# Moving the matmul operands of a two-block transformer by 32 and 160 bytes in SBUF

## The chip, the cores and the metric

One core of a Trainium2 chip runs the whole program. The metric is the device time of one execution in microseconds (us), first instruction to last with what the runtime puts around them. The kernel before took a median of 1004.35 us in three runs (1004.16 to 1005.6). SBUF is addressed here by the byte inside one partition; an "offset of 32 of 128" between two tiles means that their start addresses differ by 32 after division by 128.

## The reference, cut to what matters

The input is 256 tokens of width 1024 in float32. Block one: a norm, one wide input projection, a sparse attention over the 64 best keys and a latent attention with eight heads each, two gated branch projections, an output projection, then a feed-forward layer of width 4096 (`square(relu(h @ w_ff1)) @ w_ff2`). Block two has two layers: a windowed attention with sinks, and one that mixes compressed, selected and windowed keys; each is followed by a gated feed-forward layer of width 2816. A last norm gives the output. Nearly all arithmetic is in dense products of this form:

```python
z = h @ w_in[l]                                            # 1024 -> 3428
x = x + jnp.square(jax.nn.relu(h2 @ w_ff1[l])) @ w_ff2[l]  # 1024 -> 4096 -> 1024
gate, up = jnp.split(h @ w_gu, 2, axis=-1)                 # 1024 -> 5632, twice
return (jax.nn.silu(gate) * up) @ w_down                   # 2816 -> 1024, twice
```

## The kernel before, in words

Every dense product is done to near float32 accuracy out of three products of the faster type float32r: each operand is split into a high part and a low remainder, and `mm3` (L651 to L655) adds high times low-of-the-other, both ways, and high times high. A weight tile (128 output columns, up to eleven chunks of 128 rows) is loaded by SyncE's queue into one of four `raw` slots. ScalarE copies it rounded into one of four `w_hi` tiles (L1361), VectorE subtracts that from the raw tile into one of four `w_lo` tiles (L1988), and TensorE waits for the count of finished `w_lo` tiles. These three run as rings beside each other, with SyncE loads ahead.

In a product by features (`feature_tile`, L657) the weights are the stationary operand, 128 x 128, and the activations move, 128 x 256, in three matmuls a chunk: `w_hi` against the high activations, `w_hi` against the low ones, `w_lo` against the high ones. Each matmul has a weight load of its own, and the load for the next matmul goes on while the present one streams. The activations are `hh`/`hl` (the normalised rows, for the input, gate, query and up projections), `yh`/`yl` (attention output, for the branch and output-of-attention projections), and `hidh`/`hidl` (the hidden layer, for `w_ff2` and the first down projection; chunks of them also hold the merged branches for `w_out`). In a product by tokens (`token_tile`, L676, and `down_rows` of the last down projection) the roles are exchanged: the activations (`ch`/`cl` or `hidh`/`hidl`) are stationary and the weights move, 384 or 512 columns at a time.

Loops over passes of eight or four tiles cover the long stages (`stage_loop`). Besides, TensorE turns tiles with an identity (`ident`, L918, L940, L1210, L1316), makes attention scores (L902, L903: moving `kh`/`kl`, stationary `qs`) and multiplies probabilities (`PT` inside `big`, stationary) with values inside `work` (L930).

SBUF places follow the order in which `sb(...)` is called in `build_program`, one tensor right behind the other in multiples of 32 bytes. Those that matter, with sizes per partition: four `w_hi` and four `w_lo` of 5632 bytes each; `x` and `big`, 8192 each; `hh` and `hl`, 8192 each; then `ident`, `ones` and some forty small tensors, together 15,712 bytes with the last, `gain2`; then `work`, 91,648 bytes, under which `yh`, `yl`, `hidh`, `hidl`, `qs`, `kh`, `kl`, `xc`, `ch`, `cl` and `steps` lie at places that are multiples of 128 bytes from its start. Several short-lived tensors (`y_rows`, `c_vals`, `c_prob`) share the space of `hh` and `hl` and are declared ahead of them.

Of the kernel before, what the change touches and what calls it, by code (L numbers as in the profile page):

```python
# [24 lines left out]
P = 128  # L25
# [187 lines left out]
def build_program(nc, A, out):  # L213
    ctx = ExitStack()
    with ctx:
        def sb(name, shape, dt=F32, where=ctx):
            return where.enter_context(nc.sbuf_tensor(name, shape, dt))
# [18 lines left out]
        c_max = sb("compressed_max", [P, 2, NT * HU], where=s9)  # L236
        c_sum = sb("compressed_sum", [P, 2, NT * HU], where=s9)
        s9.close()
        hh = sb("hh", [P, KC, T], F32R)
        hl = sb("hl", [P, KC, T], F32R)  # L240
        ident = sb("ident_sb", [P, P])
# [42 lines left out]
        gain2 = sb("mid_and_attention_gain", [P, KC])  # L284


        W = 22912
        s1 = ExitStack()
        work = sb("work", [P, W], where=s1)
        s1.close()  # L290
# [35 lines left out]
        s6.close()  # L326
        ctx.enter_context(nc.sbuf_tensor("_work_place", [P, W], F32))

# [2763 lines left out]
```

## Time and profile before

| | |
|---|---|
| median of the runs | 1004.35 us (1004.16 to 1005.6) |
| the profiled execution | 1004.34 us |
| its span, first to last instruction | 1002.5 us |
| TensorE matmuls busy | 978.8 us, 98% of the span |
| VectorE, ScalarE, GpSimd busy | 691.5, 551.7, 193.9 us |
| TensorE clock granted over the span | 0.997 of full speed |
| DMA | 161.80 MB, 161 GB/s |

How to read it: PE is a matmul, PEld a weight load, which overlaps a matmul. The duration of a matmul is a modelled 280 ns or so from start to drain and matmuls overlap one another, so what a matmul costs is read from the distance between two starts, called the pitch below, and not from its duration.

### The profile page before, as it was taken

To read this page: it belongs to the slowest core of one execution; us is meant where nothing else is said; L and a number is where in the kernel's file an instruction comes from. 1 tells how busy PE (TensorE), PEld (TensorE's weight loads), DVE (VectorE), ACT (ScalarE), POOL (GpSimd) and SP (SyncE) were. 2 spreads that over 40 slices of the span, in tenths; PEclk is the share of its full clock that TensorE was granted. 3 is DMA by queue.
4 is the path that set the end of the run, shared out by engine and by line. 5 is a ranking of instruction groups with operands and counts; after the bars stand their busy time and mean duration, and the time that the engine had idled before them with its cause. 6 is when DMAs were issued, how large, how long until landed. Compare 5 with 4: busy or idle time off the path is not lost.

```text
span 1002.5 us, 21791 instructions
## 1 busy us (share of the span) xinstructions
PE 978.8 (98%) x8096; PEld 953.0 (95%) x8096; DVE 691.5 (69%) x1308; ACT 551.7 (55%) x1044; POOL 193.9 (19%) x227
## 2 busy tenths in 40 slices
PE   6999999999999999999999999999999999999997
PEld 6998999999999999998999999999999999999886
DVE  6689767777775556888666665567787866666543
ACT  6574674556663445776544454447785654454442
POOL 8000000633343433003111111220200211111000
PEclk9999999999999999999999999999999999999999
DMA  9825323545556556525667658774163476663651
GB/s 263 216 96 169 127 84 128 184 154 187 191 169 203 189 180 190 162 59 153 168 177 194 173 149 227 212 160 143 43 195 101 113 196 176 188 188 110 199 175 63
DMA packets 206004, 161.80 MB, mean 161 GB/s; under 512 B 8643, under 2 KB 193320, under 8 KB 205930
## 3 DMA queue, kind: packets, MB, share of 16 engines
q1 hardware_dynamic: 203066, 154.17, 50.9%
q0 software_dynamic: 2720, 6.56, 3.3%
q8 instruction: 49, 0.80, 0.3%
q14 instruction: 25, 0.20, 0.1%
q10 hardware_dynamic: 144, 0.07, 0.0%
HBM read 158.67 MB, written 2.10 MB: 160 GB/s over the span
## 4 chain that ended last, share of the span: by engine, by line
PE 86%; DVE 7%; ACT 3%; issue 1%; DMA 1%; SPq 1%; ACTq 0%; DVEq 0%
PE bank L653 25%; PE bank L654 25%; PE bank L655 25%; PE bank L930 3%; DVE w_lo L1988 3%; PE bank L918 2%; ACT work L1547 1%; ACT w_hi L1361 1%; PE bank L902 1%; PE bank L903 1%; PE bank L905 1%; DVE work L2198 1%; DMA raw<-w_in_in 1%; ACT big L1561 1%; PE bank L831 0%
## 5 line engine op out<-in xcount | busy, mean ns | idle before, releaser
L1988 DVE TENSOR_TENSOR w_lo<-raw,w_hi 128x1024 fp32r<-128x1024 f32 (+2 forms) x302 | 362.8, 1206 | 184.8 <-ACT w_hi L1361 182.3
L653 PE MATMUL bank<-hh,w_hi 128*128 128x256 f32 x1376 | 393.9, 286 | 4.2 <-DVE w_lo L1988 2.4
L655 PE MATMUL bank<-hh,w_lo 128*128 128x256 f32 x1376 | 389.9, 283 | 0.0
L654 PE MATMUL bank<-hl,w_hi 128*128 128x256 f32 x1376 | 389.9, 283 | 0.0
L1361 ACT ACTIVATE w_hi<-raw 128x1024 fp32r<-128x1024 f32 (+2 forms) x302 | 302.3, 1018 | 132.3 <-PE bank L655 129.6
L653 PEld LDWEIGHTS bank<-hh,w_hi 128*128 128x128 f32 x1376 | 264.0, 192 | 6.5 <-DVE w_lo L1988 5.4
L654 PEld LDWEIGHTS bank<-hl,w_hi 128*128 128x128 f32 x1376 | 264.1, 192 | 0.2
L655 PEld LDWEIGHTS bank<-hh,w_lo 128*128 128x128 f32 x1376 | 264.0, 192 | 0.0
L655 PE MATMUL bank<-hidh,w_lo 128*128 128x256 f32 x496 | 140.2, 283 | 0.0
L654 PE MATMUL bank<-hidl,w_hi 128*128 128x256 f32 x496 | 140.0, 282 | 0.0
L653 PE MATMUL bank<-hidh,w_hi 128*128 128x256 f32 x496 | 139.6, 281 | 0.0
L2940 POOL TENSOR_TENSOR hidl<-work,hidh 128x256 f32 (+1 forms) x76 | 82.3, 1083 | 278.6 <-ACT hidh L1659 278.6
L653 PEld LDWEIGHTS bank<-hidh,w_hi 128*128 128x128 f32 x496 | 94.0, 190 | 0.3
L654 PEld LDWEIGHTS bank<-hidl,w_hi 128*128 128x128 f32 x496 | 93.2, 188 | 0.0
L655 PEld LDWEIGHTS bank<-hidh,w_lo 128*128 128x128 f32 x496 | 93.0, 188 | 0.0
L1659 ACT ACTIVATE hidh<-work 128x256 f32 (+1 forms) x76 | 31.8, 419 | 73.7 <-DVE work L2479 68.8
L1547 ACT ACTIVATE work<-work,mn 128x256 f32<-128x256 f32 (+1 forms) x128 | 56.5, 448 | 5.4 <-DVE mn L2312 5.2
L653 PE MATMUL bank<-yh,w_hi 128*128 128x256 f32 x192 | 54.9, 286 | 0.7 <-DVE yl L2357 0.7
L2991 POOL MEMSET big<- 128x256 f32 x4 | 1.2, 312 | 279.8 <-DVE x L2406 206.0
L655 PE MATMUL bank<-yh,w_lo 128*128 128x256 f32 x192 | 54.2, 282 | 0.0
L654 PE MATMUL bank<-yl,w_hi 128*128 128x256 f32 x192 | 54.1, 282 | 0.0
L1653 ACT ACTIVATE work<-work 128x256 f32<-128x256 f32 x44 | 18.4, 418 | 60.6 <-DVE work L2469 60.6
(338 smaller groups left out, 1331.7 us busy)
## 6 DMA issues: line engine op xcount, KB each, us to landing
raw<-ffn_w_gu_in SPq DMA_DIRECT2D x88, 512.0 KB, 5.0
raw<-w_ff_in SPq DMA_DIRECT2D x64, 512.0 KB, 4.3
raw<-w_in_in SPq DMA_DIRECT2D x24, 512.0 KB, 5.0
raw<-ffn_w_down_in SPq DMA_DIRECT2D x44, 256.0 KB, 3.3
raw<-b_w_in_in SPq DMA_DIRECT2D x14, 512.0 KB, 6.3
raw<-ffn_w_down_in SPq DMA_DIRECT2D x16, 384.0 KB, 4.3
raw<-a_w_qkv_in SPq DMA_DIRECT2D x10, 512.0 KB, 4.6
raw<-ffn_w_down_in SPq DMA_DIRECT2D x16, 320.0 KB, 3.5
```

The source lines that it names most:

```text
L653: pe.matmul(o, ah, bh, start=start, stop=False)
L654: pe.matmul(o, ah, bl, start=False, stop=False)
L655: return pe.matmul(o, al, bh, start=False, stop=stop)
L902: pe.matmul(s_out(u, k)[:, j, :], U["q"](h), U["k"](h)[0], start=True, stop=False)
L918: mm = pe.transpose(o[:, j, c, :], s_buf[u % 2][:, h, rows * c:rows * c + rows], ident[:, :])
L930: mm = pe.matmul(psum[V_BANK][:, HD * h:HD * h + HD], PT[0:rows, h, c, :], U["v"](h, c), start=(c == 0), stop=(c == C - 1))
L1361: act.activation(tile_view(w_hi, n), raw_view(n), ACT.Copy).then_inc(hi_done, 1)
L1547: ins = act.activation(s, s, ACT.Exp, scale=-1.0, bias=mn[:, u % 3, h:h + 1], accum_out=ssum[:, u % 3, h:h + 1])
L1653: act.activation(e_buf[:, (j // 2) % 2, :], g_buf[:, (j // 2) % 2, :], ACT.Sigmoid).then_inc(e_done, 1)
L1659: act.activation(hidh[:, bass.ds(local, 1), :], v_buf[:, (j if name == "ff1" else j // 2) % 2, :].unsqueeze(1), ACT.Copy).then_inc(v_hi, 1)
L1988: dve.tensor_tensor(tile_view(w_lo, n), raw_view(n), tile_view(w_hi, n).bitcast(F32), ALU.subtract)\
L2940: pool.tensor_tensor(hidl[:, bass.ds(local, 1), :], v_buf[:, j % 2, :].unsqueeze(1), hidh[:, bass.ds(local, 1), :].bitcast(F32), ALU.subtr ...
```

## The change

Two tensors are declared that nothing reads or writes. The first, 8 floats, lies ahead of `hh` and moves `hh`, `hl` and all small tensors behind them by 32 bytes. The second, 40 floats, lies ahead of `work` and moves `work`, with all that lies in it, by 160 bytes more, 192 in all. `raw`, `w_hi`, `w_lo`, `x`, `big` and the short-lived tensors declared ahead of `hh` stay. No instruction, wait or transfer is added or taken away.

```diff
         s9.close()
+        sb("_apart_from_weight_rows", [P, 8])
         hh = sb("hh", [P, KC, T], F32R)
         hl = sb("hl", [P, KC, T], F32R)
         ident = sb("ident_sb", [P, P])
...
         gain2 = sb("mid_and_attention_gain", [P, KC])
 
 
+        sb("_work_apart_from_weight_rows", [P, 40])
         W = 22912
         s1 = ExitStack()
         work = sb("work", [P, W], where=s1)
```

## Rows read from the trace of the kernel before

**Rows 1.** Page, part 1: busy time of TensorE's two rows.
```profile
PE 978.8 (98%) x8096; PEld 953.0 (95%) x8096; DVE 691.5 (69%) x1308; ACT 551.7 (55%) x1044; POOL 193.9 (19%) x227
```

**Rows 2.** Page, part 4: the chain that ended last, by engine.
```profile
PE 86%; DVE 7%; ACT 3%; issue 1%; DMA 1%; SPq 1%; ACTq 0%; DVEq 0%
```

**Rows 3.** Waits of TensorE: line, who ended it, us in total, times, longest.
```profile
PE bank L653 <- DVE w_lo L1988: 2.4, 4, 1.4
```

**Rows 4.** Stretch: us, then PE, PEld, DVE, ACT, POOL busy (x), clock, DMA share, GB/s.
```profile
240.00:290.00 50.00, 50.00 (x419) 50.00 (x418) 36.17 (x54) 30.77 (x53) 20.43 (x17) 1.00 0.55 177
296.00:326.00 30.00, 30.00 (x251) 29.93 (x250) 16.52 (x16) 13.72 (x15) 10.02 (x11) 1.00 0.60 199
933.00:963.00 30.00, 30.00 (x130) 24.12 (x129) 13.75 (x12) 13.57 (x14) 1.14 (x1) 1.00 0.61 200
```

**Rows 5.** Matmul groups by form: count | busy us, mean ns | idle before, releaser.
```profile
L653 PE MATMUL bank<-hh,w_hi 128*128 128x256 f32 x1368 | 391.7, 286 | 4.2 <-DVE w_lo L1988 2.4 <-DVE hl L2097 1.5 <-DVE work L2534 0.2
L653 PE MATMUL bank<-hidh,w_hi 128*128 128x256 f32 x496 | 139.6, 281 | 0.0
L653 PE MATMUL bank<-yh,w_hi 128*128 128x256 f32 x192 | 54.9, 286 | 0.7 <-DVE yl L2357 0.7
L653 PE MATMUL bank<-w_hi,hidh 128*128 128x512 f32 x88 | 35.0, 398 | 0.0
```

**Rows 6.** Timeline, moving hh, 24 matmuls apart: start us, modelled duration.
```profile
250.05 0.28 PE L654 MATMUL bank<-hl,w_hi 128*128 128x256 f32 x1
...
252.93 0.28 PE L654 MATMUL bank<-hl,w_hi 128*128 128x256 f32 x1
```

**Rows 7.** Timeline, moving hidh: the 1st, 4th to 7th and 25th start.
```profile
340.53 0.28 PE L653 MATMUL bank<-hidh,w_hi 128*128 128x256 f32 x1
...
340.88 0.29 PE L653 MATMUL bank<-hidh,w_hi 128*128 128x256 f32 x1
341.01 0.28 PE L654 MATMUL bank<-hidl,w_hi 128*128 128x256 f32 x1
341.12 0.28 PE L655 MATMUL bank<-hidh,w_lo 128*128 128x256 f32 x1
341.25 0.28 PE L653 MATMUL bank<-hidh,w_hi 128*128 128x256 f32 x1
...
343.41 0.28 PE L653 MATMUL bank<-hidh,w_hi 128*128 128x256 f32 x1
```

**Rows 8.** Timeline, weights moving 384 wide against ch, 12 matmuls apart.
```profile
85.05 0.34 PE L653 MATMUL bank<-w_hi,ch 128*128 128x384 f32 x1
...
87.13 0.34 PE L653 MATMUL bank<-w_hi,ch 128*128 128x384 f32 x1
```

**Rows 9.** Timeline, scores (kh, kl against qs) behind a pause: 2nd, 10th, 16th.
```profile
704.87 0.28 PE L903 MATMUL bank<-kl,qs 128*128 128x256 f32 x1
...
705.82 0.28 PE L903 MATMUL bank<-kl,qs 128*128 128x256 f32 x1
...
706.54 0.28 PE L903 MATMUL bank<-kl,qs 128*128 128x256 f32 x1
```

**Rows 10.** Timeline, compressor, 60-column weight loads, ten matmuls apart.
```profile
732.31 0.28 PE L1177 MATMUL bank<-w_hi,xc 128*60 128x256 f32 x1
...
733.48 0.28 PE L1177 MATMUL bank<-w_hi,xc 128*60 128x256 f32 x1
```

**Rows 11.** The chain in order of time: start us, us, group; short matmuls.
```profile
700.28 0.88 PE bank L918 x8
...
706.82 3.52 PE bank L930 x32
...
931.22 1.79 PE bank L1316 x16
```

**Rows 12.** ScalarE and VectorE groups that write hh/hl and qs/kl.
```profile
L1630 ACT ACTIVATE hh<-x,cols 128x256 fp32r<-128x256 f32 x24 | 12.1, 504 | 10.3 <-DVE x L2406 5.9 <-DVE x L2408 4.3
L1726 ACT ACTIVATE qs<-work,cols 64x256 fp32r<-64x256 f32 x16 | 8.0, 503 | 4.9 <-DVE work L2534 4.7
```

## Prediction, made before the result was known

> **What bounds the kernel now.** I read the page's busy shares first: matmuls cover 98% of the span and weight loads 95% [rows 1]. The chain that ended last agrees: 86% of it is TensorE, 7% VectorE [rows 2]. Of TensorE's waits, those for a `w_lo` tile, the wait one would fear in a kernel that splits its weights on two other engines, sum to 2.4 us in four cases [rows 3]. The stretches say the same stage by stage: in 50 us of the first feed-forward product VectorE works for 36 and ScalarE for 31, while TensorE has no gap [rows 4]. So the time is set by how many matmuls there are and how far apart their starts are. The reader is not to take "98% busy" for TensorE at its best: a 256-column matmul at 2.4 GHz (the granted clock is 1.00 in these stretches) needs 256 / 2.4 = 106.7 ns of streaming. The starts of 24 matmuls on `hh` lie 252.93 - 250.05 = 2.88 us apart, which is 120.0 ns each [rows 6]. 13.3 ns a matmul, 11%, go somewhere, and only an effect on them can make this change worth anything.
>
> **How often the pitch counts.** Each of the three matmul lines has 1368 records of 128 columns on `hh`, 496 on `hidh` and 192 on `yh` [rows 5]; 2056 x 3 = 6168. With the 24 that load only 48 columns left out, that is 6168 x 0.120 = 740 us of the 1002.5 us span. One ns of pitch is 6.2 us. 0.2% of the kernel, 2 us, about what a measurement can tell from no change, is 0.32 ns of pitch. The last down projection has three lines of 88 matmuls of 512 columns [rows 5], 264 in all; one ns there is 0.26 us.
>
> **Which distances change.** Worked out from the declared sizes, modulo 128, moving address minus stationary address:
> - `hh`/`hl` against weights: the way from `w_hi` to `hh` is 8 x 5632 + 2 x 8192 = 61,440 bytes, a multiple of 128. It is 0 before and 32 after. 1368 x 3 = 4104 matmuls.
> - `hidh` and `yh` against weights: `work` starts 16,384 + 15,712 = 32,096 bytes behind `hh`, 96 beyond a multiple of 128. It is 96 before; 192 bytes more make 288, so 32 after. 688 x 3 = 2064 matmuls.
> - Weights moving against `hidh` or `ch`: 32 before, 96 after. Here the change takes away the very distance that it gives to the others.
> - Scores, `kh` against `qs`: both lie in `work`, 0 before and after.
> - Values against `PT` in `big`: 96 to 32. Identity against tiles in `work`: 32 to 0, against `x` or `y_rows`: 0 to 32.
>
> **What the distance is worth, by the trace of before.** It holds the distances 0 and 96 with activations moving, and 32 only where weights move.
> First, 0 against 96. On `hh` the pitch is 120.0 ns. On `hidh` the starts are uneven: 340.88, 341.01, 341.12, 341.25, so 0.13, 0.11, 0.13 us. But the fourth start behind 340.53 is 0.35 later and the seventh 0.72, and 24 matmuls take 343.41 - 340.53 = 2.88 us [rows 7]: again 120.0 ns. The distance moves single starts by up to 10 ns or so and the mean not at all. Counting by stretch gives the same: 419 matmuls in 50 us on `hh` and 251 in 30 us on `hidh`, where about two of each count reach in from outside [rows 4]: 50 / 417 = 119.9 ns, 30 / 249 = 120.5 ns with a short pause among them. If moving `hh` off distance 0 helped by itself, `hidh` would already show it.
> Second, distance 32. Twelve matmuls of 384 columns take 87.13 - 85.05 = 2.08 us, 173.3 ns each [rows 8]; the streaming is 384 / 2.4 = 160.0, so 13.3 ns are over. That is the same surplus as at 0 and 96 with 256 columns. The streams differ (more columns for one load), so this is a near row and no proof.
> Third, a warning that faster starts exist. Scores at distance 0 behind a pause run eight matmuls in 705.82 - 704.87 = 0.95 us, 118.8 ns, and the next six in 0.72 us, 120.0 ns [rows 9]. Products whose weight loads have 60 columns run at 1.17 / 10 = 117.0 ns with distance 32 [rows 10]. I read this as two limits: the moving stream could go on at 117 to 119 ns, and a stream of full weight loads, slowed by the moving reads beside it, settles at 120.0. A weight load without a full stream beside it needs 3.52 / 32 = 110.0 ns with values moving at distance 96, 0.88 / 8 = 110 ns for turns at distance 32 and 1.79 / 16 = 112 ns at distance 0 [rows 11]. So the load alone hardly cares for the distance, and beside a full stream it costs some 9 ns more.
>
> I take 0 ns for the 6168 matmuls, by the nearest rows: two distances with 256 columns and one with 384 all leave 13.3 ns. The bounds: below, the load's own pitch of 111 ns, 9 ns less, -56 us; above, a pitch of 125, 5 ns more and one rounding of the timeline below the widest single step in rows 7, +31 us. Neither end has a steady stretch behind it.
>
> The Trainium skill bears on this at one place, "SBUF - State Buffer", section "SBUF: two separate sides": only the port pair that VectorE and GpSimd share causes contention, and TensorE never waits on anyone; "TensorE: Matmul & The Clock Gate" adds, in its part on what happens when a matmul is issued, two independent read ports, one for the moving operand and one for weight loads. By these pages the distance could not matter, and the sum would be 0. The first half of it the trace doesn't support so plainly, since 9 ns go between the load's pitch alone and beside a full stream; that a distance changes it is shown by no row here.
>
> **The last down projection.** Its distance goes from 32 to 96. The stretch of 30 us holds 130 records [rows 4], less one or two that reach in: 30 / 128.5 = 233 ns, 20 ns over 512 / 2.4 = 213.3. The 384-column surplus of 13.3 ns is the nearest row for another value, so between -7 and +7 ns x 264: -1.8 to +1.8 us. I take 0.
>
> **Small matmuls.** Some 384 on values and 300 turns by identity run at 110 to 112 ns at all of 0, 32 and 96 [rows 11]; up to 2 ns x 700 is 1.4 us either way. I take 0.
>
> **Other engines.** ScalarE and VectorE read and write the shifted tiles too. The copy with a gain into `hh`, which starts at 0 of 128 counted from the weights, takes 504 ns, the one into `qs`, which starts at 96, 503 ns [rows 12]. So 1 ns at most, and 24 copies into `hh` make nothing of it. Every start stays a multiple of 32 bytes, so no transfer changes its packets. `raw`, `w_hi` and `w_lo` don't move, and these carry the work that follows TensorE most closely: 36 of 50 us for VectorE [rows 4]. If the pitch fell to 118, eight-chunk tiles would come every 24 x 118 = 2.83 instead of 2.88 us, still far above what VectorE needs, so a gain would not be caught there.
>
> **Sum.** 0 + 0 + 0 on the profiled execution: span 1002.5 us, 1004.3 with the 1.8 us around it. It equals the median of 1004.35.
>
> **The rivals.**
> - *Distance 32 lets the weight load past the moving stream (faster).* Then the load stops setting the pace and the moving stream does, at 117.0 [rows 10] to 118.8 ns [rows 9], say 117.9: 2.1 x 6168 = -13 us, 991 us. For it: such a pace exists, and the 60-column row that shows it is at distance 32. Against it: that row has half the load, and the 384-column row at 32 keeps its 13.3 ns. A gain on `hh` alone would be -9 us. 0.38 for this family.
> - *Distance 32 makes the starts uneven without paying back (slower).* At 96 every wide step is paid back by a narrow one, and six take 0.72 us [rows 7]. If one 10 ns step of six is not paid back, the pitch is 121.7: 1.7 x 6168 = +10 us, 1014 us. It decides from 0.32 ns of pitch. Place: every tile of every dense stage. For it: single steps do depend on the distance. Against it: no steady stretch in the trace is above 120.0. 0.17.
> - *The change does less than it says.* Scores stay at 0, the 512-column products go from 32 to 96. This ends inside no change, at -1.8 to +1.8 us, and is in its chance.
>
> **How the numbers follow.** No change 0.45, faster 0.38, slower 0.17. The time is that of no change, 1004.3 us; its own range is 1002.3 to 1006.3. Down, the range takes in the faster rival with its larger variants, to a pitch of 117.0: 3.0 x 6168 = 18.5 us, 986 us. Up it reaches to 1010 us, a pitch of 120.9, which takes in the milder part of the slower rival and not its priced middle. About 0.05 is left below and 0.1 above.
>
> **What would show it right or wrong.** Right: 24 matmuls on `hh`, and 24 on `hidh`, still take 2.88 us; the groups of rows 5 keep their counts, and stretches as long as those of rows 4 hold 417 and 249 starts. Faster: 24 take 2.83 us or less in both stages, and the chain keeps its TensorE share of 86%. A change of `hh` alone would mean that 0 is the bad distance. Slower: 24 take over 2.89 us with steps of 125 ns. Wrong in its whole argument: the pitch keeps to 120.0 and the time moves by more than 2 us, for then the difference lies in waits at stage changes, and [rows 3] would show other lines.

## The result, and the profile after

The changed kernel takes a median of 987.01 us (986.34 to 988.08, four runs) beside 1004.3 us before (1004.16 to 1005.6, four runs): 17.3 us less, a ratio of 0.983 with a 95% interval of 0.981 to 0.984. The span of its profiled execution is 986.3 us, 16.2 us less than before. The forecast was no change, 1004.3 us; the faster rival, given 0.38, was the one that came. The time lies inside the stated range of 986 to 1010 us, one us from its lower end, which was there for that rival's largest variant.

The page of the changed kernel: the busy shares, then the chain that ended last by engine. They answer to [rows 1] and [rows 2]; every line number behind the two strips is higher by 1 or 2.

```profile
PE 961.3 (97%) x8096; PEld 935.3 (95%) x8096; DVE 690.9 (70%) x1308; ACT 551.7 (56%) x1044; POOL 195.3 (20%) x227
PE 86%; DVE 7%; ACT 3%; issue 1%; DMA 1%; SPq 1%; ACTq 0%; DVEq 0%
```

The counts are the same, 8096 matmuls and as many weight loads, and the engines beside TensorE are each as busy as they were to 1.4 us. Only TensorE's two rows fell, the matmuls by 17.5 us and the weight loads by 17.7. So the same instructions stand closer together.

The stretches of the changed kernel (us, then PE, PEld, DVE, ACT, POOL busy with counts, clock, DMA share, GB/s), against [rows 4]:

```profile
235.00:285.00 50.00, 50.00 (x431) 50.00 (x431) 37.30 (x54) 31.20 (x54) 21.29 (x19) 1.00 0.58 189
296.00:326.00 30.00, 30.00 (x256) 29.85 (x256) 16.31 (x17) 12.57 (x13) 11.63 (x12) 1.00 0.66 211
917.00:947.00 30.00, 30.00 (x131) 24.14 (x130) 13.94 (x12) 13.80 (x15) 1.15 (x1) 1.00 0.63 203
```

In 50 us on `hh` there are 431 records where there were 419, in 30 us on `hidh` 256 where there were 251, and in the last down projection 131 where there were 130. The granted clock is 1.00 in all, as before.

The timeline shows the pitch itself. First two starts on `hh` that are 24 matmuls apart, then two on `hidh` 24 apart, then two with weights moving 384 wide, 12 apart; they answer to [rows 6], [rows 7] and [rows 8]:

```profile
245.31 0.28 PE L655 MATMUL bank<-hh,w_hi 128*128 128x256 f32 x1
...
248.11 0.28 PE L655 MATMUL bank<-hh,w_hi 128*128 128x256 f32 x1
...
599.93 0.28 PE L655 MATMUL bank<-hidh,w_hi 128*128 128x256 f32 x1
...
602.73 0.28 PE L655 MATMUL bank<-hidh,w_hi 128*128 128x256 f32 x1
...
84.66 0.34 PE L655 MATMUL bank<-w_hi,ch 128*128 128x384 f32 x1
...
86.74 0.34 PE L655 MATMUL bank<-w_hi,ch 128*128 128x384 f32 x1
```

24 matmuls take 2.80 us instead of 2.88 in both: 116.7 ns each instead of 120.0. The 384-column products keep their 2.08 us, although their distance went from 32 to 96 of 128. The scores stay at 120 ns, eight starts in 693.79 - 692.83 = 0.96 us, and the 60-column loads at 117 ns, 1.17 us for ten; rows that answer to [rows 9] and [rows 10]:

```profile
692.83 0.28 PE L905 MATMUL bank<-kl,qs 128*128 128x256 f32 x1
...
693.79 0.28 PE L905 MATMUL bank<-kl,qs 128*128 128x256 f32 x1
...
719.60 0.28 PE L1179 MATMUL bank<-w_hi,xc 128*60 128x256 f32 x1
...
720.77 0.28 PE L1179 MATMUL bank<-w_hi,xc 128*60 128x256 f32 x1
```

Averaged over all steady stretches (starts with no pause in between) the pitch is 116.7 ns on `hh`, 117.0 on `hidh` and 117.1 on `yh`, where all three had 120.0; the 512-column products went from 234.2 to 233.3.

**The ledger.** 4104 x 3.3 + 1488 x 3.0 + 576 x 2.9 + 264 x 1.0 ns = 13.5 + 4.5 + 1.7 + 0.3 = 20.0 us. The span fell by 16.2. The two traces have the same matmuls in the same order, so the distances between starts can be compared one by one: the steady stretches gained 17.2 us and the short runs of matmuls 1.8, while 1.0 was lost near the start to the clock and 1.9 to longer waits and pauses. First the clock. Stretches of before, then of after:

```profile
30.00:36.00 6.00, 6.00 (x111) 5.78 (x111) 5.69 (x13) 2.93 (x8) 1.17 (x2) 0.81 0.91 218
31.00:32.00 1.00, 1.00 (x46) 1.00 (x43) 1.00 (x2) 0.98 (x3) 0.00 (x0) 1.00 0.80 217
37.00:38.00 1.00, 1.00 (x10) 1.00 (x10) 0.00 (x0) 0.83 (x2) 0.00 (x0) 0.93 0.93 96
```
```profile
30.00:36.00 6.00, 6.00 (x107) 5.90 (x107) 5.69 (x13) 2.82 (x7) 1.17 (x2) 0.60 0.92 221
31.00:32.00 1.00, 1.00 (x43) 1.00 (x40) 1.00 (x2) 0.98 (x2) 0.00 (x0) 0.57 0.81 205
37.00:38.00 1.00, 1.00 (x6) 1.00 (x6) 0.00 (x0) 0.00 (x0) 0.00 (x0) 0.52 0.98 94
```

From 30.1 to 32.4 us TensorE runs 90 very short matmuls for the bias table, with 33 of 128 rows in use, and in both executions its clock drops from 2.4 to 1.2 GHz for a while. In the changed kernel the low level lasts from 31.1 us, in the middle of these matmuls, to 38.0; before it lasted from 33.7, behind them, to 37.1. The mean granted clock of the 6 us is 0.60 instead of 0.81. The 250th matmul starts at 35.3 us instead of 34.4. It need not be owed to the change: the four executions of the changed kernel have a mean granted clock of 0.995, 0.995, 0.997 and 0.997, for the kernel before it ranges from 0.994 to 1.000, one execution at 0.989 apart, and the kernel with both at 64, below, has no drop there in its profile. About 1.1 us more goes into waits for weights:

```profile
PE bank L655 <- DVE w_lo L1990: 3.5, 6, 1.4
```

It was 2.4 us in four waits [rows 3]; the other 0.8 us is in many smaller ones. The last 1 us of the difference to the ledger is a price set too high: the ledger gives every matmul the gain of a steady stretch, and the short runs of matmuls, many of them between attention steps, gained less.

### The profile page after: what moved, and what is told of

It is laid out like the page before. It is cut to its first block, busy times and chain, and to the rows that moved or that the text cites. A ratio compares the mean times of both kernels' runs of the same rounds, so it can differ in the third digit from the quotient of the medians.

```text
span 986.3 us, 21791 instructions
## 1 busy us (share of the span) xinstructions
PE 961.3 (97%) x8096; PEld 935.3 (95%) x8096; DVE 690.9 (70%) x1308; ACT 551.7 (56%) x1044; POOL 195.3 (20%) x227
## 4 chain that ended last, share of the span: by engine, by line
PE 86%; DVE 7%; ACT 3%; issue 1%; DMA 1%; SPq 1%; ACTq 0%; DVEq 0%
PE bank L655 25%; PE bank L657 24%; PE bank L656 24%; PE bank L932 4%; DVE w_lo L1990 3%; PE bank L920 2%; ACT work L1549 1%; ACT w_hi L1363 1%; PE bank L904 1%; PE bank L905 1%; PE bank L907 1%; DMA raw<-w_in_in 1%; DVE work L2200 1%; ACT big L1563 1%; PE bank L833 0%
## 5 line engine op out<-in xcount | busy, mean ns | idle before, releaser
L655 PE MATMUL bank<-hh,w_hi 128*128 128x256 f32 x1376 | 389.4, 283 | 5.1 <-DVE w_lo L1990 3.1
L657 PE MATMUL bank<-hh,w_lo 128*128 128x256 f32 x1376 | 385.1, 280 | 0.0
L656 PE MATMUL bank<-hl,w_hi 128*128 128x256 f32 x1376 | 385.0, 280 | 0.0
L655 PEld LDWEIGHTS bank<-hh,w_hi 128*128 128x128 f32 x1376 | 259.4, 188 | 7.4 <-DVE w_lo L1990 6.2
L656 PEld LDWEIGHTS bank<-hl,w_hi 128*128 128x128 f32 x1376 | 259.4, 189 | 0.2
L657 PEld LDWEIGHTS bank<-hh,w_lo 128*128 128x128 f32 x1376 | 259.2, 188 | 0.0
```

The source lines that it names most:

```text
L655: pe.matmul(o, ah, bh, start=start, stop=False)
L656: pe.matmul(o, ah, bl, start=False, stop=False)
L657: return pe.matmul(o, al, bh, start=False, stop=stop)
```

## The experiments

Every kernel here is the kernel before with other strips; the operations are the same in all. "Distance" is moving minus stationary start address. Where two numbers stand, the first is for `hh`/`hl`, the second for `hidh`, `hidl`, `yh` and `yl` against the weights.

**Only `hh` moved.**
```diff
+        sb("_apart_from_weight_rows", [P, 8])
         hh = sb("hh", [P, KC, T], F32R)
...
+        sb("_work_apart_from_weight_rows", [P, 24])
         W = 22912
```


> Strip of 32 bytes ahead of hh, and one of 96 bytes ahead of work, so that hh and hl lie 32 of 128 off the weights and work stays at 96. Theory A (the distance between moving and stationary operand, modulo 128, sets the pace of each product by itself): the products on hh go to a pitch of 116.7 ns and those on hidh and yh stay at 120.0; 4104 x 3.3 ns = 13.5 us, less the 10 to 15% that waits give back: 991 to 993 us. Theory B (the gain is one of hidh and yh, or needs both groups moved, e.g. by what ScalarE and VectorE do beside the stream): hh stays at 120.0 or moves by under 1 ns, time over 998 us.

990.35 us, ratio 0.986 (0.984 to 0.988), 14.0 us less than before and 0.65 us below what was expected. `hh` ran at 116.7 ns in most stages (mean 117.0). So most of the gain is `hh`'s alone, as Theory A had it. But `hidh`, which kept its 96 of 128, did not stay at 120.0. Its timeline, 24 matmuls apart:

```profile
599.93 0.28 PE L655 MATMUL bank<-hidh,w_hi 128*128 128x256 f32 x1
...
602.77 0.28 PE L655 MATMUL bank<-hidh,w_hi 128*128 128x256 f32 x1
```

2.84 us, 118.3 ns. To keep `work` at 96 of 128 the strips had moved it by 128 bytes, and that was enough. Modulo 128 is the wrong measure.

**Only `work` moved.**
```diff
+        sb("_work_apart_from_weight_rows", [P, 48])
         W = 22912
```


> Only a strip of 192 bytes ahead of work: hidh, hidl, yh, yl, kh, kl and qs where the changed kernel has them modulo 128, hh and hl at distance 0 as before. Theory A: hidh and yh at 116.7 to 117.8 ns, hh at 120.0; 2064 x 3 ns = 6 us, time 998 to 999.5 us, and together with the kernel that moves hh alone the gains add up to that of the change (17 us). Theory B (the two groups gain only together): within 1 us of 1004.3.

1000.12 us, ratio 0.996 (0.994 to 0.997), 4.2 us less, 0.6 us short of what was expected. `hh` at 120.0, `hidh` at 117.5 in the mean, `yh` at 116.7. The two parts give 14.0 + 4.2 = 18.2 us, the whole change 17.3. That they come so near is no clean sum: in the first, `hidh` and `yh` gained 1.7 ns too, worth 1.7 x 2064 = 3.5 us, while `hh` was 0.35 ns slower in the mean than in the changed kernel, 1.4 us.

**Both at 64.**
```diff
+        sb("_apart_from_weight_rows", [P, 16])
         hh = sb("hh", [P, KC, T], F32R)
...
+        sb("_work_apart_from_weight_rows", [P, 8])
         W = 22912
```


> hh/hl and work both at 64 of 128 off the weights. Theory A1 (the farther from the weight's own line the better; 32 is just off 0): pitch at or below 116.7 ns, time 985 to 988 us or less. Theory A2 (only a band around 32 is good, since 96, which is 32 the other way, has 120.0): pitch 120.0 in both groups, time 1003 to 1005 us.

986.45 us, ratio 0.982 (0.980 to 0.985), no different from the change. Two starts on `hh`, 24 apart:

```profile
245.47 0.28 PE L655 MATMUL bank<-hh,w_hi 128*128 128x256 f32 x1
...
248.29 0.28 PE L655 MATMUL bank<-hh,w_hi 128*128 128x256 f32 x1
```

2.82 us: `hh` ran at 117.8 ns nearly everywhere, slower than at 32, so A1 ("the farther the better") falls and A2 ("only 32") as well. The time is inside what A1 gave, 985 to 988 us, but by luck: `hidh`, at 448 of 512, ran in some passes at 117.8 and in others at 113.3 ns, faster than anything before it. `hh` had that pace too, in one short run of 70 matmuls; 24 of them apart:

```profile
74.00 0.28 PE L655 MATMUL bank<-hh,w_hi 128*128 128x256 f32 x1
...
76.72 0.28 PE L655 MATMUL bank<-hh,w_hi 128*128 128x256 f32 x1
```

**Everything moved together.**
```diff
+        sb("_ahead_of_weights", [P, 8])
         w_hi = [sb(f"w_hi{i}", [P, TILE_EL], F32R) for i in range(HL)]
```


> A strip of 32 bytes ahead of w_hi, so that the weight tiles, x, big, hh and work all move by 32 bytes and every distance is that of the kernel before (0 and 96). Theory A (distance): pitch 120.0 everywhere, 1003.5 to 1005 us. Theory C (the absolute start of the moving tile decides: hh now starts 32 further, as in the changed kernel): hh at about 116.7 ns, time about 991 us.

1004.84 us, ratio 1.000 (0.999 to 1.001); 120.0 ns on `hh`, `hidh` and `yh`. The start of `hh` moved by the same 32 bytes as in the changed kernel, and nothing changed. It is the distance to the weights that counts and not the address. Theory C is out. `raw` stayed where it was, so the distance to it doesn't count either.

**Is the period 128, 256 or 512?** Three kernels, one execution each.

```diff
+        sb("_apart_from_weight_rows", [P, 24])
...
+        sb("_work_apart_from_weight_rows", [P, 104])
```


> hh at 96 of 512 bytes off the weights (96 of 128, where hidh was before), hidh and yh at 352 of 512, as before. Theory A (distance modulo 128 decides): hh at 120.0 ns as hidh was at 96, so nothing is gained on hh: 1003 to 1005 us. Theory D (a longer period, 256 or 512, decides, because moving hh alone brought hidh from 120.0 to 118.3 when work was moved by just 128 bytes): hh is free to differ from 120.0, in one of the steps seen (113.3, 116.7, 117.8, 118.3); hidh stays at 120.0, which would make the period a divisor of 512.

```diff
+        sb("_apart_from_weight_rows", [P, 88])
...
+        sb("_work_apart_from_weight_rows", [P, 96])
```


> The places are exchanged: hh at 352 of 512, where hidh was before, hidh and yh at 64, where hh was in the kernel with both at 64. Theory D (the distance alone decides and not which tile it is or what stage it runs in): hh 120.0 ns, hidh and yh 117.8 ns; 2064 x 2.2 = 4.5 us, about 1000 us. Theory F (the stage and its neighbours on other engines decide): hidh keeps 113.3 or goes elsewhere, hh is not at 120.0.

```diff
+        sb("_apart_from_weight_rows", [P, 32])
...
+        sb("_work_apart_from_weight_rows", [P, 8])
```


> hh at 128 of 512, hidh and yh at 0. Theory A (modulo 128): both 120.0 ns, 1004 us. Theory D: hidh and yh at 120.0 as hh was at 0, hh may differ: by under 120.0 if the period is over 128. With 117.8 on hh: 995 to 997 us.

They took 1004.7, 1001.57 and 997.89 us. The first and the third on `hh`, 24 matmuls apart:

```profile
245.41 0.28 PE L655 MATMUL bank<-hh,w_hi 128*128 128x256 f32 x1
...
248.29 0.28 PE L655 MATMUL bank<-hh,w_hi 128*128 128x256 f32 x1
```
```profile
245.20 0.28 PE L655 MATMUL bank<-hh,w_hi 128*128 128x256 f32 x1
...
248.05 0.28 PE L655 MATMUL bank<-hh,w_hi 128*128 128x256 f32 x1
```

At 96 it is 2.88 us, 120.0 ns, what `hidh` had at 352; at 352 `hh` has 120.0 too. At 64 of 512 `hidh` has 117.8 ns, as `hh` had at 64: the tile and its stage don't matter, and Theory F falls. At 128 `hh` takes 2.85 us, 118.7 ns, and not the 120.0 of distance 0: a period of 128 is out. 96 and 352 agree, and so do 192 and 448 (`hidh` in the kernel with both at 64 and in the one with both at 192) and, with 512 columns moving, 64 and 320, both at 228.9 ns: 256 fits every pair that I have. The other distances were not run 256 bytes apart. The third kernel also has the fastest 512-column products, with weights moving at distance 0 to `hidh`, 15 matmuls apart:

```profile
930.36 0.39 PE L655 MATMUL bank<-w_hi,hidh 128*128 128x512 f32 x1
...
933.76 0.39 PE L655 MATMUL bank<-w_hi,hidh 128*128 128x512 f32 x1
```

3.40 us, 226.7 ns by these two rows and 226.9 over all, instead of 234.2. The second kernel took 1.6 us more than expected (about 1000 us), the third 0.9 us more (995 to 997 us, at 117.8 on `hh`).

**The last distances.**
```diff
+        sb("_apart_from_weight_rows", [P, 40])
...
+        sb("_work_apart_from_weight_rows", [P, 32])
```


> The last distances of the 32-byte grid: hh at 160 of 256, hidh and yh at 128. Theory D: hidh and yh run at 118.7 ns, which hh had at 128; hh at 160 is new: if the pace depends on the distance smoothly, between 118.7 (128) and the 113.3 to 117.7 of 192, so 116 to 118 ns. Time 990 to 996 us.

```diff
+        w_room = sb("w_room", [P, 2 * HL * TILE_EL + 8], F32R)
+        w_hi = [w_room[:, 4 + i * TILE_EL:4 + (i + 1) * TILE_EL] for i in range(HL)]
+        w_lo = [w_room[:, 4 + (HL + i) * TILE_EL:4 + (HL + i + 1) * TILE_EL] for i in range(HL)]
...
+        sb("_apart_from_weight_rows", [P, 40])
...
+        sb("_work_apart_from_weight_rows", [P, 48])
```


> The weight rings start 16 bytes into a room of their own, so that hh lies 176 of 256 bytes off them and hidh/yh 208: 16 bytes to either side of 192, where the pitch was 113.3 ns in some passes and 117.7 in others, changing only at the pause of a loop's branch. Theory D (distance modulo 256 decides, in steps coarser than 16 bytes): the same two paces as at 192 on both. Rival G (distance matters to 16 bytes): one of them holds one pace throughout; with 113.3 on hh alone 4104 x 6.7 = 27 us, time 972 to 978 us; with 118 on both 990 to 993 us.

996.35 and 999.2 us. This pair was made after the kernel with both at 192, below. Beside them the kernel before took 1012.37 us in its one execution, at a granted clock of 0.989, 8 us more than elsewhere, so the pitches are compared here and not the times. `hidh` at 128: 118.7 ns, as expected. `hh` at 160 had several paces, 117.3 to 120.0 ns by stage; I had expected 116 to 118. 16 bytes off 192 both expectations fail (999.2 us is above all times that they gave): `hh` at 176 ran at 118.7 ns throughout, `hidh` and `yh` at 208 at 117.8 in some stages and at 123.3 in others, the slowest steady pitch of all. Two starts on `yh`, 24 apart; the weight tiles bear their room's name:

```profile
164.89 0.29 PE L656 MATMUL bank<-yh,w_room 128*128 128x256 f32 x1
...
167.85 0.29 PE L656 MATMUL bank<-yh,w_room 128*128 128x256 f32 x1
```

2.96 us, 123.3 ns. So 16 bytes matter, and 192 may be narrow. A rival stands: these are also the only weight tiles that start off a multiple of 32 bytes, and no run separates that from the distance.

The pitch by distance modulo 256, all kernels together:

| distance | 256 columns move, full weight load | 512 columns move |
|---|---|---|
| 0 | 120.0 (before; 128/0 kernel) | 226.9 |
| 32 | 116.7 to 117.8 (the change) | 233.3 |
| 48 | not run | 233.3 |
| 64 | 117.8; 113.3 in 70 matmuls | 228.9 |
| 96 | 120.0 (before; 96/352, 352/64 kernels) | not run |
| 128 | 118.7 | 232.8 |
| 160 | 117.3, 118.7 or 120.0 | 234.2 (before) |
| 176 | 118.7 | not run |
| 192 | 113.3 or 117.8 | 233.3 |
| 208 | 117.8 or 123.3 | not run |
| 224 | 118.3 | 233.3 (the change) |

**Both at 192.**
```diff
+        sb("_apart_from_weight_rows", [P, 112])
         hh = sb("hh", [P, KC, T], F32R)
...
+        sb("_work_apart_from_weight_rows", [P, 104])
         W = 22912
```


> hh at 448 of 512 (64 short of the weights' line), where hidh was when the fastest steady pitch so far, 113.3 ns, appeared in part of its stages; hidh and yh at 192. Theory D: hh runs at 117.8 ns in some stages and at 113.3 in others, mean between; 4104 x (2.2 to 6.7) = 9 to 27 us for hh, and with hidh at 118 another 4: 975 to 993 us. Theory F (113.3 belongs to the stages of hidh): hh 117.8, 991 to 994 us.

981.96 us in the median, but from 976.7 to 988.84, ratio 0.980 (0.976 to 0.984). The timeline of its `ff2` stage has two paces, 24 matmuls apart each, in one stage on one tile pair:

```profile
308.08 0.28 PE L655 MATMUL bank<-hidh,w_hi 128*128 128x256 f32 x1
...
310.91 0.28 PE L655 MATMUL bank<-hidh,w_hi 128*128 128x256 f32 x1
...
315.95 0.28 PE L655 MATMUL bank<-hidh,w_hi 128*128 128x256 f32 x1
...
318.67 0.28 PE L655 MATMUL bank<-hidh,w_hi 128*128 128x256 f32 x1
```

2.83 us, 117.9 ns, and then 2.72 us, 113.3 ns. Between them, at 313 us, two steps take 0.20 and 0.22 us instead of 0.12; I take them for the loop's branch. A pace holds for dozens of matmuls and changes at such a pause, up or down. One change has no pause: at 180 us `hidh` goes from 117.8 to 113.3 ns, and the longest step there is 0.13 us. The first feed-forward product ran at 117.8 in this execution, the up projections at 113.3. `hh` does have 113.3, so it isn't `hidh`'s own.

**Change and 192 side by side**, five executions of the one and six of the other on one chip:

> The changed kernel once more, beside the next one on one chip: 986 to 989 us, ratio to before 0.981 to 0.984, scatter within 2 us, since its pitch hardly changes between passes (116.7 ns, here and there 117.8).

> hh at 448 and hidh/yh at 192 of 512 (both 192 of 256) once more. If the pause at a loop's branch picks one of two paces (113.3 or 117.7 ns) from run to run, the times scatter over 977 to 989 us with a median near 982, 4 to 6 us under the changed kernel; if the fast first run was the exception and 117.7 is the rule, the median is 987 to 989 us, no better than the changed kernel.

The changed kernel: 987.29 us (986.97 to 988.2), ratio 0.983 (0.982 to 0.984). Both at 192: 976.69 us (974.67 to 984.13), ratio 0.973 (0.971 to 0.976), 5 us under my expectation; in its profiled execution 71% of the steady matmuls on `hh` had the fast pace. It beats both kernels, the changed one by 10.6 us, with ranges that don't overlap, at the price of a scatter of 9.5 us where the changed kernel has 1.2. Two stretches of 40 us on `hh`, in the changed kernel and in this one:

```profile
480.00:520.00 40.00, 40.00 (x345) 40.00 (x344) 27.48 (x44) 19.96 (x30) 7.57 (x8) 1.00 0.71 197
```
```profile
480.00:520.00 40.00, 40.00 (x355) 40.00 (x354) 29.48 (x47) 19.85 (x30) 7.12 (x8) 1.00 0.69 190
```

343 starts in one and 353 in the other, two records of each count reaching in from outside: 116.6 and 113.3 ns.

## Why the prediction was wrong, and where it was right

**The range held, the forecast did not.** 987.01 us is inside 986 to 1010, but the central value, no change with 0 ns, missed by 17.3 us. What saved the range is that it reached down to a pitch of 117.0 for the rival.

**What bounds the kernel: right.** The pitch of the dense products sets the time, one ns is about 6 us, and a gain there passes to the end. The three kernels with one, the other and both groups moved gave 14.0, 4.2 and 17.3 us; the chain kept its 86%.

**The step that failed** is "I take 0 ns for the 6168 matmuls, by the nearest rows: two distances with 256 columns and one with 384 all leave 13.3 ns." It measured 3.3 ns on `hh`, 3.0 on `hidh` and 2.9 on `yh`. Three things were wrong in it.
- The distances were worked out modulo 128, after the change's own words, although nothing in the trace gives that number. The period is 256. The two distances of before, 0 and 96 of 256, happen to be the only two on the 32-byte grid at which every run had 120.0 ns. I drew a flat line through two points of a curve.
- The argument "if moving `hh` off distance 0 helped by itself, `hidh` would already show it" took `hidh` as a test of "not 0". It was a test of 96 only; the uneven steps in [rows 7] said that the distance acts on single starts, and more weight was given to the equal mean.
- The row of 384 columns was read as evidence for 32 because its surplus was 13.3 ns too. The runs show that such rows don't carry over. Modulo 256 its distance was 160 before and 224 after. It kept 173.3 ns when its own distance changed, and in the 512-column products the best distance is 0, which with 96 is the slowest of the 32-byte grid for 256 columns. With another ratio of moving to stationary bytes the curve is another.

**The faster rival: right in its direction and its pace, low in size.** It said that the pace goes to that of the scores behind a pause and of the 60-column loads, 117.9 ns, and priced 991 us; it was 116.7 to 117.1 ns and 987. It priced `hh` alone at -9 us, as if the other products gained on their own; `hh` alone gave the larger part of 14.0. That the load is what the stream holds up was argued and is not shown: no run separates a delayed load from a delayed stream, and why some distances are fast stays open. What is shown is that address distance, with all operations equal, moves the pitch between 113.3 and 120.0 ns (to 123.3 with the weight tiles 16 bytes off), while the weight load without a full stream beside it takes 110 to 112 ns [rows 11].

**The slower rival** did not come, but a pitch above 120.0 exists: at 208 a stage sits at 123.3 ns. In the range the upper end was for it.

**The last down projection, small matmuls, other engines: right at 0.** 1.0 ns x 264 = 0.3 us; VectorE, ScalarE and GpSimd are busy for 0.6 us less, as long, and 1.4 us more. The scores stayed at a distance of 0 and at 120 ns. In the part on what would show it, the line "24 take 2.83 us or less in both stages, and the chain keeps its TensorE share of 86%" is what came.

The Trainium skill, "SBUF - State Buffer", section "SBUF: two separate sides", says that TensorE never waits on anyone. The trace disagrees as far as TensorE's own two streams go: with nothing but addresses changed, 24 matmuls take 2.88, 2.80 or 2.72 us. The prediction's remark that 9 ns go between the load's pitch alone and beside a full stream, which it held against the page, was the better guide.

## What to carry to other kernels

Where TensorE bounds a kernel and its pitch is clearly above the streaming time, try the distance between moving and stationary tiles before anything costly: two spare strips of 32 to 448 bytes per partition each gave 1.7 to 2.7% here, with no instruction changed. Scan it, modulo at least 256 bytes and at the column counts that the kernel uses; two distances with the same pitch say nothing about a third. And look at the scatter: a distance may have a fast and a slow pace and change between them at a pause.

## What the runs showed of the hardware that was not expected

- The pitch of 256-column float32r matmuls with a 128-column weight load each takes fixed values: 113.3, 116.7, 117.8, 118.3, 118.7, 120.0, 123.3 ns. Times 2.4 GHz (the granted clock is 1.00 there), 113.3, 116.7, 120.0 and 123.3 are 272, 280, 288 and 296 cycles, all multiples of 8; the others are none.
- Single steps differ by some 10 ns in a pattern that repeats, while 24 matmuls of one pace take the same time to the 0.01 us of the timeline.
- At distance 192 two paces, 113.3 and 117.8 ns, exist side by side, and at 64, as far on the other side of 0, the same two; two steps of 0.2 us can switch them. The kernel that has them scatters by 9.5 to 12 us, its other versions by under 5 us.
- Around the 90 short matmuls the clock fell to 1.2 GHz in all profiled executions but one, in some during them (from 31.1 us in the changed kernel, 31.4 in its second profile), in others behind them (33.7 before). The longer stretch cost about 1 us. With both at 64 it did not fall there. Such differences are part of the scatter of one kernel: among thirteen executions of the kernel before, the two at a granted clock of 0.999 took 1002.67 and 1002.78 us and the longest, at 0.995, 1005.65. What decides it the runs don't tell.
